# Mixer B's intra-chunk products: six halving levels in place of token pairs and far blocks

## The chip, the cores and the metric

The kernel runs on one core of a Trainium2 chip. The metric is device time in microseconds (us) for one launch; everything is float32. TensorE multiplies, VectorE (DVE) and ScalarE (ACT) work element by element, GpSimd has little to do, and SyncE's queue (SP) issues nearly all loads.

## The reference, cut to what matters

Two layers (`DEPTH`), each with 1024 tokens and 1024 channels. One projection of the normalised input feeds four token mixers A to D; their outputs are projected, weighted by gates, summed and added to the residual. The change is inside mixer B alone, a gated linear recurrence with 4 heads of 64 channels, in chunks of 64 tokens:

```
bcum = cumsum(log_f) inside the chunk
att[t, s] = sum_d q[t, d] * k[s, d] * exp(bcum[t, d] - bcum[s, d])      for s <= t
o = att @ v + (q * exp(bcum)) @ state
state = exp(b_last) * state + (k * exp(b_last - bcum))^T @ v
```

The exponent depends on the token pair and on the channel, so `att` is no plain product of two matrices. It becomes one if a reference position r with s <= r <= t is put between: exp(bcum[t] - bcum[r]) scales q and exp(bcum[r] - bcum[s]) scales k, and both factors are at most 1.

## The kernel before, in words

**Order of the work.** The mixers run in the order C, D, B, A, each with a stream of instructions per engine; a stage of B begins on TensorE when D's outputs have been turned. The heads of B are worked in two halves m (two heads e each, on partitions 64e to 64e+63); chunks c lie in pairs, one tile i of 128 tokens (8 tiles).

**Filler.** `pe_fill(pe, n)` puts n matmuls of later projections (128x128 weights, 512 columns; each matmul is two instructions in the trace, L368 and L365) into TensorE's queue between dependent steps. The list `FILL_ORDER` is fixed and in order: projections for D, gate blocks, projections for B, more gate blocks, projections for A, gate blocks. 8 matmuls make a piece, which ScalarE copies out of one of two PSUM banks; 4 pieces make a block of weights, which SyncE loads two blocks ahead. What is left of the list when mixer A ends is run at the start of the last stage (`pe_tail`, L456). `D_FILL`, `B_FILL` and `ATT_FILL` say how many matmuls stand at each place. In B they are 16 three times ("start"), then in each half 3 before each of 16 pair steps, 1 ("near"), 1 ("far"), 2 and 1 in each of 8 tiles, and at last 16 ("turn"), 212 in all.

**Mixer B before.** After VectorE's running sums (`log_cum`) each half goes through these steps:
1. Pairs within 16 tokens. For each offset s in 0..15 VectorE subtracts (L1272), ScalarE exponentiates (L1197), VectorE multiplies by q and k (L1290, L1292) over 1024 - 64 s elements, in two buffers `ee`, and TensorE sums over the channels with a selector matrix (L1099). ScalarE copies the sums (L1199), TensorE transposes them.
2. State additions. VectorE scales the keys to the chunk's end (L1295, L1297), TensorE transposes them (L1116), ScalarE copies (L1207), TensorE multiplies with the values (L1123), VectorE runs a chain of 15 steps for the states (L1304).
3. For each tile VectorE places the pair sums (L1316), TensorE brings them into PSUM with the identity (L1133) and adds the far blocks of 16 tokens (L1137), VectorE masks (L1321), TensorE multiplies with the values (L1147) and adds the product of queries and state (L1150), ScalarE copies (L1210).

At the end VectorE normalises and gates (L1327 to L1335) and TensorE turns the result (L560). Mixer A begins with `pe_fill_until`, then its projection (L341); its VectorE part first waits for a bias table that SyncE builds by three DMAs in turn, once B has ended (L798 to L803).

Of the kernel before, what the change touches and what calls it, by code (L numbers as in the profile page):

```python
# [8 lines left out]
ALU = mybir.AluOpType  # L9
# [10 lines left out]
SUB = 16  # L20
NSUB = CH // SUB
# [22 lines left out]
B_FILL = {"start": 16, "pairs": 3, "far": 1, "attT": 2, "oB": 1, "turn": 16, "near": 1}  # L44
# [9 lines left out]
for _n, _w in PARAM_SIZES:  # L54
# [3 lines left out]
CONST_SIZES = [("ident", 128), ("head_sum", 128), ("pair_sel", 62), ("strict_c", 64),  # L58
               ("incl_t", 128), ("incl_c", 64), ("lv0", 64), ("lv1", 64), ("lv2", 64), ("lv3", 64), ("lv4", 64), ("lv5", 64),
               ("lv0_t", 64), ("sub_diag", 128), ("chunk_neg", 128), ("rot", 128), ("ones", 64), ("diag2", 64)]  # L60
# [6 lines left out]
def constants():  # L67
# [12 lines left out]
    put("pair_sel", np.concatenate([np.zeros((P, 30)), (t // HD) == np.arange(2)[None, :], np.zeros((P, 30))], 1))  # L80
    put("incl_t", same & (s >= t))
# [6 lines left out]
    put("sub_diag", ((t // SUB) == (s // SUB)) & (s <= t))  # L88
# [78 lines left out]
def gated_merge_kernel(nc, x, w_in, w_branch, w_out, params, toep, consts, cos_sin, a_mask, final_g, out):  # L167
    ctx = ExitStack()
    jobs = Jobs()
    with ctx:  # L170
# [886 lines left out]
        def mixer_b():  # L1057
            q, key, bc, v, z = bq_raw, U(0), bf_raw, b_v, V(2)
            o_rows = H(14.5, 2).rearrange("p (m i c) -> p m i c", m=2, i=NT)
            qt, qh, kj = H(4), H(5), [H(6), H(7), H(8)]  # L1060
            khn = H(9).rearrange("p (i c) -> p i c", i=NT)
            ee = [H(10), H(11)]
            near = H(12, 0.25).rearrange("p (i j e) -> p i e j", i=NT, e=2)
            st = H(12.5, 1.0625).rearrange("p (c v) -> p c v", c=17)
            near_x = H(12.25, 0.25).rearrange("p (e s) -> p e s", e=2)
            att_t = [H(13.5625 + 0.25 * n, 0.25).rearrange("p (e t) -> p e t", e=2) for n in range(2)]
# [14 lines left out]
            def subs(x):  # L1081
                return x.rearrange("p (c j t) -> p c j t", j=NSUB, t=SUB)

            def pe(pe):
# [4 lines left out]
                for m in range(2):  # L1089

                    ap = jobs.open(pe, ("near", m), S2[0])
                    for s in range(SUB):
                        pe_fill(pe, B_FILL["pairs"])
                        pe.wait_ge(sg("pairs_ready"), SUB * m + s + 1)
                        for half in range(2):

                            x = ee[s % 2][:, 512 * half:512 * half + 512].rearrange("p (b t) -> p b t", t=SUB)[:, :, s:]
                            o = ap[0:2 * SUB, 512 * half:512 * half + 512].rearrange("p (b t) -> p b t", t=SUB)[:, :, s:]
                            ins = pe.matmul(o, lhsT=C("pair_sel")[:, 2 * (SUB - 1 - s):2 * (2 * SUB - 1 - s)], rhs=x,  # L1099
                                            start=s == 0, stop=True, skip_group_check=True)  # L1100
                        jobs.mark(("pairs", m, s))
                        if s < SUB - 1:
                            ins.then_inc(sg("pairs_summed"), 1)
                    jobs.filled(ins, ("near", m))
                    pe_fill(pe, B_FILL["near"])
                    jobs.stored(pe, ("near", m))
                    ap = jobs.open(pe, ("nearT", m), O)
                    for i in range(NT):
                        ins = pe.transpose(ap[:, 2 * SUB * i:2 * SUB * i + 2 * SUB], ee[1][0:2 * SUB, P * i:P * i + P],
                                           ident[0:2 * SUB, 0:2 * SUB])  # L1110
                    jobs.filled(ins, ("nearT", m))

                    ap = jobs.open(pe, ("khn", m), S2[1])
                    pe.wait_ge(sg("end_keys"), m + 1)
                    for i in range(NT):
                        ins = pe.transpose(ap[:, P * i:P * i + P], ee[0][:, P * i:P * i + P], ident)  # L1116
                    jobs.filled(ins, ("khn", m))
                    jobs.stored(pe, ("khn", m))
# [7 lines left out]
                    pe_fill(pe, B_FILL["far"])  # L1126
                    pe.wait_ge(sg("far_ready"), m + 1)
                    for i in range(NT):
                        pe.wait_ge(sg("near_placed"), NT * m + i + 1)
                        ap = jobs.open(pe, ("attT", m, i), S2[0])  # L1130
                        for e in range(2):
                            o = ap[:, 512 * e:512 * e + P]
                            pe.matmul(o, lhsT=near_x[:, e, :], rhs=ident, start=True, stop=True, skip_group_check=True)  # L1133
                            for j in range(1, NSUB):
                                cols = o.rearrange("p (c j t) -> p c j t", c=2, j=NSUB)[:, :, j, :]
                                rhs = subs(qt)[HD * e:HD * e + HD, 2 * i:2 * i + 2, j, :]
                                ins = pe.matmul(cols, lhsT=kj[j - 1][HD * e:HD * e + HD, P * i:P * i + P], rhs=rhs,  # L1137
                                                start=False, stop=True, skip_group_check=True)
                        jobs.filled(ins, ("attT", m, i))
                        pe_fill(pe, B_FILL["attT"])  # L1140
                        if i == 0:
                            pe.wait_ge(sg("states_" + str(m)), 1)
                        jobs.stored(pe, ("attT", m, i))
                        ap = jobs.open(pe, ("oB", m, i), S2[1])
                        for e in range(2):
                            vv = v[:, i, HD * (2 * m + e):HD * (2 * m + e) + HD]
                            pe.matmul(ap[:, 512 * e:512 * e + HD], lhsT=att_t[i % 2][:, e, :], rhs=vv, start=True, stop=True, skip_group_check=True)  # L1147
                            for c in range(2):
                                t0 = P * i + CH * c
                                ins = pe.matmul(ap[CH * c:CH * c + CH, 512 * e:512 * e + HD], lhsT=qh[HD * e:HD * e + HD, t0:t0 + CH],  # L1150
                                                rhs=st[HD * e:HD * e + HD, 2 * i + c, :], start=False, stop=True, skip_group_check=True)
                        jobs.filled(ins, ("oB", m, i))
                        pe_fill(pe, B_FILL["oB"])
# [4 lines left out]
            def act(act):  # L1158
# [22 lines left out]
                for m in range(2):  # L1181
                    b = bc[:, m, :]
                    if m:
                        act_ready(act, ("oB", 0, NT - 1))
                    act.activation(qh, b, ACT.Exp).then_inc(sg("qh_exp"), 1)
                    act.wait_ge(sg("qt_diff"), m + 1)
                    act.activation(subs(qt)[:, :, 1:, :], subs(qt)[:, :, 1:, :], ACT.Exp).then_inc(sg("qt_exp"), 1)
                    for j in range(1, NSUB):
                        act.wait_ge(sg("kj_diff"), 3 * m + j)
                        x = chunks(kj[j - 1])[:, :, 0:SUB * j]  # L1190
                        act.activation(x, x, ACT.Exp).then_inc(sg("kj_exp"), 1)
                    for s in range(SUB):
                        if s >= 2:
                            act_fills(act, ("pairs", m, s - 2))
                        act.wait_ge(sg("pair_diff"), SUB * m + s + 1)
                        x = ee[s % 2].rearrange("p (b t) -> p b t", t=SUB)[:, :, s:]
                        act.activation(x, x, ACT.Exp).then_inc(sg("pair_exp"), 1)  # L1197
                    ap = act_ready(act, ("near", m))
                    jobs.emptied(act.activation(ee[1][0:2 * SUB, :], ap[0:2 * SUB, :], ACT.Copy), ("near", m))  # L1199
                    ap = act_ready(act, ("nearT", m))  # L1200
                    if m:
                        jobs.ready(act, ("attT", 0, NT - 1))
                    jobs.emptied(act.activation(H(12, 0.25), ap[:, 0:256], ACT.Copy), ("nearT", m))
                    act.wait_ge(sg("end_diff"), m + 1)
                    act.activation(ee[0], ee[0], ACT.Exp).then_inc(sg("end_exp"), 1)
                    ap = act_ready(act, ("khn", m))
                    jobs.emptied(act.activation(H(9), ap, ACT.Copy), ("khn", m))  # L1207
                    for i in range(NT):
                        ap = act_ready(act, ("oB", m, i))
                        jobs.emptied(act.activation(o_rows[:, m, i, :].rearrange("p (e v) -> p e v", e=2),  # L1210
                                                    ap.rearrange("p (e v) -> p e v", e=2)[:, :, 0:HD], ACT.Copy), ("oB", m, i))
# [5 lines left out]
            def dve(dve):  # L1217
# [34 lines left out]
                for m in range(2):  # L1252
                    b, qq, kk = bc[:, m, :], q[:, m, :], key[:, m, :]

                    if m:
                        jobs.ready(dve, ("oB", 0, NT - 1))
# [615 lines left out]
```

## Time and profile before

| what | value |
|---|---|
| median of 3 runs | 3810.22 us (3809.53 to 3810.95) |
| the profiled execution's own time | 3809.59 us |
| its span | 3807.8 us |
| mean granted TensorE clock | 0.960 of 2.4 GHz |
| TensorE busy | 3507.4 us (92%) |
| VectorE busy | 1695.2 us (45%) |
| ScalarE busy | 690.3 us (18%) |
| GpSimd busy | 60.9 us (2%) |

The span is the time from the first to the last instruction; the execution's time is 1.8 us longer. A busy TensorE isn't TensorE at its peak, since its clock has two levels and small products leave most of the array idle.

### The profile page before, as it was taken

How to read it: one execution, taken by the hardware profiler on the slowest of the kernel's cores; microseconds unless marked ns; L12 is line 12 of the kernel's file. 1: busy time of each engine (PE TensorE's matmuls, PEld its weight loads, DVE VectorE, ACT ScalarE, POOL GpSimd, SP SyncE). 2: the span in 40 equal slices, each digit the busy share in tenths (PEclk: the TensorE clock that was granted, in tenths of full speed). 3: DMA queues.
4: the chain of work that ended last, by engine and by line, in shares of the span. 5: the costliest groups of instructions: out<-in, count | busy, mean ns of one | idle time of the engine just before them, and what ended most of it. 6: DMA issues, size and time to landing. Idle time of an engine off the chain costs nothing. (4 is left out here: it accounts for less than half of the span.)

```text
span 3807.8 us, 42754 instructions
## 1 busy us (share of the span) xinstructions
PE 3507.4 (92%) x17400; PEld 1764.5 (46%) x17400; DVE 1695.2 (45%) x3604; ACT 690.3 (18%) x1334; POOL 60.9 (2%) x52
## 2 busy tenths in 40 slices
PE   7999979999998998999989999789999899899997
PEld 3343545455543453554443345454555344546443
DVE  1179952722365321226112899446323734212442
ACT  2031023200122111310111310232101312113000
POOL 0003000000000000000000110000000000000000
PEclk9999989999998999999999999999999889899999
DMA  4101110100010012035031011000011101020531
GB/s 165 36 11 45 52 40 17 33 13 26 29 59 25 25 39 86 28 120 176 0 114 36 23 38 65 23 20 31 13 32 40 42 28 42 30 82 25 185 108 50
DMA packets 132334, 195.53 MB, mean 51 GB/s; under 512 B 8072, under 2 KB 87976, under 8 KB 131880
## 3 DMA queue, kind: packets, MB, share of 16 engines
q1 hardware_dynamic: 113544, 158.67, 12.9%
q10 hardware_dynamic: 18592, 34.09, 2.5%
q8 instruction: 140, 2.29, 0.3%
q14 instruction: 58, 0.48, 0.0%
HBM read 146.07 MB, written 48.78 MB: 51 GB/s over the span
## 5 line engine op out<-in xcount | busy, mean ns | idle before, releaser
L368 PE MATMUL ps<-hT,wr 128*128 128x512 f32 x3008 | 1445.0, 619 | 28.0 <-DMA wr<-in_w_in 10.4
L368 PEld LDWEIGHTS ps<-hT,wr 128*128 128x128 f32 x3008 | 549.7, 195 | 613.6 <-issue 573.1
L1031 DVE TENSOR_SCALAR_CACHE_REDUCE arena<-arena,sm 128x384 f32<-128x384 f32 (+5 forms) x384 | 337.9, 943 | 2.2
L758 DVE CUSTOM_DVE_ANT_0 arena<-ps,arena 128x640 f32<-128x640 f32 (+7 forms) x128 | 90.6, 708 | 373.8 <-PE ps L702 373.7
L341 PE MATMUL ps<-wr,hT 128*128 128x512 f32 x512 | 225.0, 601 | 15.2 <-DVE arena L629 15.2
L325 PE MATMUL ps<-hT,wr 128*128 128x512 f32 x512 | 224.6, 600 | 0.0
L466 PE MATMUL ps<-xo,arena 128*128 128x512 f32 x512 | 220.2, 592 | 1.7 <-ACT gts L408 1.7
L478 PE MATMUL ps<-wr,hT 128*128 128x512 f32 x512 | 220.1, 592 | 0.0
L1438 PEld LDWEIGHTS ps<-arena 64*64 64x64 f32 x4096 | 139.2, 135 | 135.0 <-issue 65.2
L365 PE MATMUL ps<-wr,hT 128*128 128x256 f32 (+1 forms) x512 | 192.2, 510 | 6.5 <-DMA wr<-in_w_in 6.5
L715 PEld LDWEIGHTS ps<-arena 128*128 128x128 f32 x1056 | 137.2, 193 | 82.0 <-issue 76.0
L408 ACT ACTIVATE gts<-ps 128x512 f32<-128x512 f32 x128 | 76.0, 596 | 507.5 <-PE ps L368 507.1
L1438 PE MATMUL ps<-arena 64*64 64x64 f32 (+1 forms) x4096 | 165.1, 227 | 0.0
L341 PEld LDWEIGHTS ps<-wr,hT 128*128 128x128 f32 x512 | 98.9, 194 | 141.3 <-issue 124.4
L325 PEld LDWEIGHTS ps<-hT,wr 128*128 128x128 f32 x512 | 98.3, 193 | 127.0 <-issue 127.0
L466 PEld LDWEIGHTS ps<-xo,arena 128*128 128x128 f32 x512 | 97.1, 190 | 124.8 <-issue 124.8
L478 PEld LDWEIGHTS ps<-wr,hT 128*128 128x128 f32 x512 | 97.3, 190 | 122.5 <-issue 122.5
L737 ACT ACTIVATE arena<-arena,sm 128x640 f32<-128x640 f32 (+7 forms) x128 | 94.1, 735 | 302.6 <-DVE sm L763 302.6
L715 PE MATMUL ps<-arena 128*128 128x64 f32 x1056 | 134.3, 271 | 11.0 <-DVE arena L775 9.8
L692 PE MATMUL ps<-con,arena 128*128 128x128 f32 x528 | 99.1, 292 | 41.7 <-ACT arena L737 34.9
L365 PEld LDWEIGHTS ps<-wr,hT 128*128 128x128 f32 x512 | 90.6, 191 | 39.6 <-issue 27.4
L1099 PE MATMUL ps<-arena,con 128*32 128x512 f32 (+15 forms) x256 | 78.1, 430 | 30.2 <-DVE arena L1292 30.0
(270 smaller groups left out, 3245.9 us busy)
## 6 DMA issues: line engine op xcount, KB each, us to landing
wr<-in_w_in SPq DMA_DIRECT2D x68, 1024.0 KB, 5.7
gate_tanh<-gts ACTq DMA_DIRECT2D x128, 256.0 KB, 2.0
arena<-gate_tanh SPq DMA_DIRECT2D x128, 256.0 KB, 2.9
x_cur<-arena SPq DMA_DIRECT2D x2, 4096.0 KB, 17.0
arena<-in_w_branch SPq DMA_DIRECT2D x8, 1024.0 KB, 8.7
wr<-in_w_out SPq DMA_DIRECT2D x8, 1024.0 KB, 6.1
arena<-x_cur SPq DMA_DIRECT2D x4, 2048.0 KB, 8.0
arena<-in_x SPq DMA_DIRECT2D x4, 1024.0 KB, 7.9
```

Source lines behind the costliest of these rows:

```text
L325: ins = pe.matmul(ap, lhsT=wr[:, n % 2, kt, P * m:P * m + P], rhs=hT[:, kt, 512 * half:512 * half + 512], start=kt == 0, stop=kt == KT - 1)
L341: ins = pe.matmul(o, lhsT=hT[:, kt, P * i:P * i + P], rhs=wr[:, n % 2:n % 2 + nb, kt, :], start=kt == 0, stop=kt == KT - 1)
L365: ins = pe.matmul(ap[:, 0:NCB * nb].rearrange("p (a c) -> p a c", a=nb), lhsT=hT[:, kt, P * c:P * c + P], rhs=wr[:, slot:slot + nb, kt, :] ...
L368: ins = pe.matmul(ap, lhsT=wr[:, slot, kt, P * m:P * m + P], rhs=hT[:, kt, 512 * c:512 * c + 512], start=kt == 0, stop=kt == KT - 1)
L466: ins = pe.matmul(ap, lhsT=wbs[ORDER.index(b)][:, k2, P * ct:P * ct + P], rhs=xo[:, 2 * ORDER.index(b) + k2, 512 * half:512 * half + 512], ...
L478: ins = pe.matmul(ap[:, 512 * j:512 * j + 512].rearrange("p (a c) -> p a c", a=2), lhsT=yT[:, kt, P * i:P * i + P], rhs=wr[:, 2 * j:2 * j ...
L692: ins = pe.transpose(ap[:, P * j:P * j + P], rows[u % 2][:, P * (g + j):P * (g + j) + P], ident)
L715: ins = pe.matmul(o[:, HD * h:HD * h + HD], lhsT=probs_t[u % 2][:, P * j:P * j + P], rhs=v[:, k0 + j, HD * h:HD * h + HD], start=j == 0, s ...
L737: act.activation(r, r, ACT.Exp, bias=neg[:, u % 2:u % 2 + 1], accum_out=tot[:, u % 8:u % 8 + 1]).then_inc(sg("probs_" + b), 1)
L758: ins = dve.tensor_tensor_reduce(out=rows[u % 2][:, 0:P * nb], in0=ap[:, 0:P * nb], in1=bias(i, h, nb), scale=HD ** -0.5, scalar=-3e38, op ...
L1031: ins = dve.tensor_scalar(compared[i], iscore[i], cbits[:, j:j + 1], None, ALU.is_ge, ALU.add, accum_out=count[:, j:j + 1])
L1438: ins = pe.matmul(ap[rows, c0 + width * h:c0 + width * h + width], lhsT=left[rows, h, :], rhs=right[rows, h, :], start=True, stop=True)
```

## The change

The chunk of 64 tokens is halved six times (`LEVELS = 6`). At level n it lies in blocks of 2h tokens, h = 32, 16, 8, 4, 2, 1. With the block's last token of the first half as reference, the second half of q and the first half of k are scaled and lie side by side in one buffer of 1024 columns, `scaled[n]`. The product of the buffer with itself, 64x64 for each head and chunk, has the pairs (s in the first half, t in the second half of one block) among others that a mask removes. A seventh product of plain keys and queries gives the diagonal. VectorE masks all seven (`near7`) and sums over them into `att_t`. TensorE keeps the output of all 8 tiles in two PSUM banks (`T`, `O`, one per head): first the products of queries and states, then for each tile the values. ScalarE copies each bank once per half. The end keys come first now, with their own buffer `ek`. TensorE's loop over the tiles puts in turn: the seven products of tile i, one matmul of filler, the values of tile i - 1. Filler in B is 3 x 16, in each half 6 + 2 + 16 and 8 x 1, and 16 at the end: 128 in all.

```diff
-B_FILL = {"start": 16, "pairs": 3, "far": 1, "attT": 2, "oB": 1, "turn": 16, "near": 1}
+B_FILL = {"start": 16, "end": 6, "khn": 2, "adds": 16, "att": 1, "turn": 16}
+            scaled = [H(4 + n) for n in range(LEVELS)]
+            qh, ek = H(10), H(12)
+            def second(x, lv):
+                return x.rearrange("p (b n t) -> p n b t", n=2, t=CH >> (lv + 1))[:, 1]
...
             def pe(pe):
...
                 for m in range(2):
+                    pe_fill(pe, B_FILL["end"])
+                    ap = jobs.open(pe, ("khn", m), S2[1])
+                    pe.wait_ge(sg("end_keys"), m + 1)
+                        ins = pe.transpose(ap[:, P * i:P * i + P], ek[:, P * i:P * i + P], ident)
+                    pe_fill(pe, B_FILL["khn"])
...
+                    pe_fill(pe, B_FILL["adds"])
+                    pe.wait_ge(sg("qh_ready"), m + 1)
+                    pe.wait_ge(sg("states_" + str(m)), 1)
...
+                    pe.wait_ge(sg("scaled_ready"), m + 1)
+                    for i in range(NT + 1):
+                        if i < NT:
+                            ap = jobs.open(pe, ("att", m, i), S2[i % 2])
+                            for n in range(LEVELS + 1):
+                                left, right = (scaled[n], scaled[n]) if n < LEVELS else (key[:, m, :], q[:, m, :])
+                                for e in range(2):
+                                    for c in range(2):
+                                        d, t0, c0 = slice(HD * e, HD * e + HD), P * i + CH * c, 512 * e + CH * n
+                                        ins = pe.matmul(ap[CH * c:CH * c + CH, c0:c0 + CH], lhsT=left[d, t0:t0 + CH],
+                                                        rhs=right[d, t0:t0 + CH], start=True, stop=True)
+                            pe_fill(pe, B_FILL["att"])
+                        pe.wait_ge(sg("att_ready"), NT * m + i)
...
              def act(act):
...
                 for m in range(2):
+                    act.activation(ek, ek, ACT.Exp).then_inc(sg("end_exp"), 1)
+                    for n in range(LEVELS):
+                        act.wait_ge(sg("level_diff"), LEVELS * m + n + 1)
+                        act.activation(scaled[n], scaled[n], ACT.Exp).then_inc(sg("level_exp"), 1)
+                        if n == 1:
+                            ap = act_ready(act, ("khn", m))
+                            jobs.emptied(act.activation(H(11), ap, ACT.Copy), ("khn", m))
+                            act.activation(qh, bc[:, m, :], ACT.Exp).then_inc(sg("qh_exp"), 1)
 ...
             def dve(dve):
...
                 for m in range(2):
+                    def level_diff(n):
+                        half = CH >> (n + 1)
+                        mid = b.rearrange("p (b t) -> p b t", t=2 * half)[:, :, half - 1:half].broadcast_to([P, S // (2 * half), half])
+                        dve.tensor_tensor(second(scaled[n], n), second(b, n), mid, ALU.subtract)
+                        dve.tensor_tensor(first(scaled[n], n), mid, first(b, n), ALU.subtract).then_inc(sg("level_diff"), 1)
+                    for n in range(LEVELS):
+                        if n + 1 < LEVELS:
+                            level_diff(n + 1)
+                        dve.wait_ge(sg("level_exp"), LEVELS * m + n + 1)
+                        dve.tensor_tensor(second(scaled[n], n), second(scaled[n], n), second(qq, n), ALU.mult)
+                        ins = dve.tensor_tensor(first(scaled[n], n), first(scaled[n], n), first(kk, n), ALU.mult)
+                    dve.tensor_tensor(qh, qh, qq, ALU.mult).then_inc(sg("qh_ready"), 1)
...
                     for i in range(NT):
+                        ap = jobs.ready(dve, ("att", m, i))
...
+                        ins = dve.tensor_tensor(masked, ap.rearrange("p (e n t) -> p e n t", e=2, t=CH)[:, :, 0:LEVELS + 1], each, ALU.mult)
+                        jobs.emptied(ins, ("att", m, i))
+                        jobs.stored(dve, ("att", m, i))
...
+                        dve.tensor_reduce(att_t[i % 2], masked.rearrange("p e n t -> p e t n"), AX, ALU.add).then_inc(sg("att_ready"), 1)
```

## Rows read from the trace of the kernel before

**Rows 1.** The page's busy times: engine, us, share of the span, instructions.
```profile
PE 3507.4 (92%) x17400; PEld 1764.5 (46%) x17400; DVE 1695.2 (45%) x3604; ACT 690.3 (18%) x1334; POOL 60.9 (2%) x52
```

**Rows 2.** Stretches: us, busy time of each engine (instructions), PEclk, DMA share, GB/s.
```profile
1107.20:1443.88 336.68, 306.63 (x1161) 151.85 (x1161) 150.31 (x237) 70.47 (x108) 0.00 (x0) 0.91 0.10 34
2984.51:3321.21 336.70, 306.68 (x1162) 151.87 (x1161) 150.29 (x237) 70.46 (x108) 0.00 (x0) 0.91 0.10 34
...
1220.00:1240.00 20.00, 12.65 (x105) 9.01 (x105) 7.52 (x21) 3.96 (x5) 0.00 (x0) 0.59 0.04 14
```

**Rows 3.** The filler of L368 alone in the first of these stretches.
```profile
1107.20:1443.88 336.68, 208.15 (x424) 77.69 (x424) 0.91 0.10 34
```

**Rows 4.** TensorE in order of time: start us, us, instructions; the last stage's filler.
```profile
1666.55 20.77 PE L368 MATMUL ps<-hT,wr 128*128 128x512 f32 x48
```

**Rows 5.** TensorE in order of time in mixer B, [idle before <-releaser].
```profile
1107.20 45.90 PE L368 MATMUL ps<-hT,wr 128*128 128x512 f32 x102
1158.43 3.62 PE L1099 MATMUL ps<-arena,con 128*32 128x512 f32 x4 [5.33 <-DVE arena L1292]
...
1227.87 1.99 PE L1123 MATMUL ps<-xo,arena 64*64 64x64 f32 x64 [1.11 <-ACT arena L1207]
...
1235.28 0.77 PE L1133 MATMUL ps<-con,arena 128*128 128x128 f32 x2 [3.42 <-DVE arena L1316]
```

**Rows 6.** The page's groups: busy us, mean ns of one, idle before.
```profile
L1438 PE MATMUL ps<-arena 64*64 64x64 f32 (+1 forms) x4096 | 165.1, 227 | 0.0
...
L1099 PE MATMUL ps<-arena,con 128*32 128x512 f32 (+15 forms) x256 | 78.1, 430 | 30.2 <-DVE arena L1292 30.0
```

**Rows 7.** TensorE in order of time in mixer D, one tile's products.
```profile
837.73 0.85 PE L1411 MATMUL ps<-con,arena 128*128 128x128 f32 x6 [1.14 <-DVE arena L1645]
838.51 0.46 PE L1422 MATMUL ps<-arena 64*64 64x64 f32 x16
838.79 0.41 PE L1422 MATMUL ps<-xo,arena 64*64 64x64 f32 x16
...
840.90 1.98 PE L365 MATMUL ps<-wr,hT 128*128 128x512 f32 x4
842.82 1.15 PE L1438 MATMUL ps<-arena 64*64 64x64 f32 x32
```

**Rows 8.** ScalarE in order of time in mixer B: copies of transposes and of a tile.
```profile
1226.79 1.02 ACT L1207 ACTIVATE arena<-ps 128x1024 f32<-128x1024 f32 x1 [3.38 <-PE ps L1116]
...
1263.52 0.28 ACT L1210 ACTIVATE arena<-ps 128x128 f32<-128x128 f32 x1 [5.95 <-PE ps L1150]
```

**Rows 9.** VectorE in order of time in mixer B: the states, the normalisation.
```profile
1229.99 4.71 DVE L1304 SCALAR_TENSOR_TENSOR arena<-arena,sm,ps 128x64 f32<-128x64 f32 x15 [5.25 <-PE ps L1123]
...
1429.61 2.29 DVE L1327 TENSOR_TENSOR arena<-arena 128x2048 f32<-128x2048 f32 x1 [2.87 <-ACT arena L1210]
...
1439.78 2.36 DVE L1335 TENSOR_TENSOR arena<-arena 128x1024 f32<-128x1024 f32 x2
```

**Rows 10.** VectorE's groups by shape: busy us, mean ns, idle before.
```profile
L1328 DVE TENSOR_REDUCE sm<-arena 128x32 f32<-128x2048 f32 x1 | 2.3, 2286 | 0.0
...
L1292 DVE TENSOR_TENSOR arena<-arena 128x512 f32<-128x512 f32 x1 | 0.7, 691 | 0.0
...
L1292 DVE TENSOR_TENSOR arena<-arena 128x256 f32<-128x256 f32 x1 | 0.4, 425 | 0.0
...
L1292 DVE TENSOR_TENSOR arena<-arena 128x64 f32<-128x64 f32 x1 | 0.3, 275 | 0.0
```

**Rows 11.** The start of mixer A in order of time, TensorE and VectorE.
```profile
1450.95 7.77 PE L368 MATMUL ps<-hT,wr 128*128 128x512 f32 x12
...
1476.46 3.03 DVE L821 SCALAR_TENSOR_TENSOR arena<-arena 128x640 f32<-128x640 f32 x4 [34.32 <-DMA arena<-a_bias_table]
...
1479.87 43.10 PE L341 MATMUL ps<-wr,hT 128*128 128x512 f32 x96 [7.42 <-DVE arena L629]
```

**Rows 12.** TensorE in order of time in mixer D: filler after its weights.
```profile
924.93 2.05 PE L368 MATMUL ps<-hT,wr 128*128 128x512 f32 x2 [5.26 <-DMA wr<-in_w_in]
```

More of the change, by code:

```diff
@@ L19 @@
 CH = 64
-SUB = 16
-NSUB = CH // SUB
+LEVELS = 6
 HD = 64
@@ L79, in constants @@
     put("head_sum", same)
-    put("pair_sel", np.concatenate([np.zeros((P, 30)), (t // HD) == np.arange(2)[None, :], np.zeros((P, 30))], 1))
-    put("incl_t", same & (s >= t))
     tc, sc = t % CH, np.arange(CH)[None, :]
@@ L87, in constants @@
         put(f"lv{lv}", ((tc // (2 * b)) == (sc // (2 * b))) & ((tc // b) % 2 == 1) & ((sc // b) % 2 == 0))
-    put("sub_diag", ((t // SUB) == (s // SUB)) & (s <= t))
+    halves = [CH >> (n + 1) for n in range(LEVELS)]
+    put("near7", np.concatenate([((tc // (2 * b)) == (sc // (2 * b))) & ((tc // b) % 2 == 0) & ((sc // b) % 2 == 1)
+                                 for b in halves] + [tc == sc], 1))
     put("chunk_neg", np.where((t // CH) < (s // CH), -BIG, 0.0))
@@ L1059, in mixer_b @@
             o_rows = H(14.5, 2).rearrange("p (m i c) -> p m i c", m=2, i=NT)
[L1060 to L1066, printed above, removed]
+            scaled = [H(4 + n) for n in range(LEVELS)]
+            qh, ek = H(10), H(12)
+            khn = H(11).rearrange("p (i c) -> p i c", i=NT)
+            st = H(13, 1.0625).rearrange("p (c v) -> p c v", c=17)
+            att_t = [H(14.0625 + 0.125 * n, 0.125).rearrange("p (e t) -> p e t", e=2) for n in range(2)]
+            masked = H(21.25, 0.875).rearrange("p (e n t) -> p e n t", e=2, n=LEVELS + 1)
             bc_flat = H(16.5, 2)
@@ L1089, in pe @@
                 for m in range(2):
[L1091 to L1111, printed above, removed]
+                    pe_fill(pe, B_FILL["end"])
+                    jobs.mark(("B end", m))
                     ap = jobs.open(pe, ("khn", m), S2[1])
@@ new lines, in pe @@
+                    pe_fill(pe, B_FILL["adds"])
+                    jobs.mark(("B adds", m))
+                    o = [jobs.open(pe, ("oB", m, e), bk) for e, bk in enumerate((T, O))]
+                    pe.wait_ge(sg("qh_ready"), m + 1)
+                    pe.wait_ge(sg("states_" + str(m)), 1)
+                    for i in range(NT):
+                        for c in range(2):
+                            t0 = P * i + CH * c
+                            for e in range(2):
+                                ins = pe.matmul(o[e][CH * c:CH * c + CH, CH * i:CH * i + CH], lhsT=qh[HD * e:HD * e + HD, t0:t0 + CH],
+                                                rhs=st[HD * e:HD * e + HD, 2 * i + c, :], start=i == 0, stop=True, skip_group_check=True)
@@ L1181, in act @@
                 for m in range(2):
[L1182 to L1199, printed above, removed]
@@ L1212, in act @@
+                    act_fills(act, ("B adds", m))
+                    for i in range(NT):
+                        act_fills(act, ("B att", m, i))
+                    for e in range(2):
+                        ap = act_ready(act, ("oB", m, e))
+                        ins = act.activation(o_rows[:, m, :, HD * e:HD * e + HD], ap.rearrange("p (i v) -> p i v", i=NT), ACT.Copy)
+                        jobs.emptied(ins, ("oB", m, e))
                 act.wait_ge(sg("b_square"), 1)
@@ new lines, in dve @@
+                    r = chunks(b)[:, :, CH - 1:CH].broadcast_to([P, NCH, CH])
+                    dve.tensor_tensor(chunks(ek), r, chunks(b), ALU.subtract).then_inc(sg("end_diff"), 1)
+                    level_diff(0)
+                    dve.wait_ge(sg("end_exp"), m + 1)
+                    dve.tensor_tensor(ek, ek, kk, ALU.mult).then_inc(sg("end_keys"), 1)
+                    for n in range(LEVELS):
[4 more added lines that the diff above has]
+                        ins = dve.tensor_tensor(first(scaled[n], n), first(scaled[n], n), first(kk, n), ALU.mult)
```

127 lines of the change are left out of this document (32 added, 95 removed).

## The prediction

> **What bounds the kernel now.** I read the page's busy times first, then the stretches of mixer B, then the order in which TensorE works there, then the other engines at the places where it waits.
>
> TensorE is busy for 92% of the span and VectorE for 45% [rows 1], so TensorE's queue sets the time and I price only what shortens or lengthens that queue. Mixer B is the stretch from the end of mixer D's turns to the start of B's own: 336.68 us in the first layer, 336.70 us in the second [rows 2]. One layer is worked out and doubled.
>
> Much of B is filler: 424 instructions of later projections [rows 3], two to each call counted by `pe_fill`. At the higher level of the clock one takes 0.43 us (48 in 20.77 us [rows 4]), so 424 are 182 us; the trace has 208 us, because part of them ran at the lower clock. The other 155 us of B (336.7 minus 182) are B's own products, waits, and time at the lower clock. Around 1220 to 1240 us the granted clock averages 0.59 of 2.4 GHz and TensorE is idle for 7 of 20 us [rows 2]. The waits are on VectorE's pair products and then on its chain of states, 5.33 us and 3.42 us in the shown half [rows 5]. The pair sums alone are 256 instructions and 78.1 us in both layers [rows 6]. In the loop over tiles one tile takes 6.2 us (0.28 + 5.95 us between ScalarE's copies [rows 8]): VectorE masks, TensorE multiplies, each waiting for the other, with filler between.
>
> **What goes, per layer.** All pair sums (39 us), the transposes of their result, the far products and the masks at full width. The 336.7 us are replaced as a whole, so nothing is subtracted twice.
>
> **What comes, per layer, in TensorE's order.** The filler of the opening is kept: 102 instructions took 45.9 us [rows 5], of which the last 6 stood ahead of the first pair sums. The new opening has 12 ("end") in their place: 45.9 + 6 x 0.43 = 48.5 us.
>
> Each half m then has:
> - 8 transposes of the scaled end keys. Six took 0.78 us to the next start [rows 7], so 1.0 us.
> - 2 fills, 1.7 us. ScalarE's copy of the transposes takes 1.02 us [rows 8] and lies beside them.
> - 32 products that add to the states, 64 instructions. The price is that of mixer D's 64x64 products which go around all four quarters of the array: 16 instructions in 0.28 us, 0.0175 us each [rows 7]. 1.1 us, and 0.2 us for the change from filler to 64x64 (four instructions of filler, 1.72 us at 0.43, took 1.92 us to the next start [rows 7]): 1.3 us.
> - 16 fills, 13.8 us, to hide VectorE's work. VectorE is held at level 2, whose exponential stands behind the copy and `qh`'s on ScalarE: about 3.2 us after the transposes, by three instructions over 1024 elements, some 1.02 us each [rows 8]. Behind it are six pairs of 512-wide operations (two 0.69 us operations overlap to 1.22 us [rows 10]), 7.3 us, `qh` 1.1 us and the chain of 15 states 4.7 us [rows 9]: 16.3 us after the transposes. TensorE arrives after 1.7 + 1.3 + 13.8 = 16.8 us. Level 5 works on single elements; by the reading below that may add up to 1.5 us. I put 1.0 us of waiting into the sum (bounds 0 and 2).
> - 32 products of queries with states, 1.1 + 0.2 = 1.3 us.
> - The loop over 8 tiles, below: 24.6 us.
>
> That is 1.0 + 1.7 + 1.3 + 13.8 + 1.0 + 1.3 + 24.6 = 44.7 us, twice 89.4 us. The second half also has 6 fills of "end", 5.2 us; the first half's are in the opening. The turns come last: 16 fills, 13.8 us. VectorE's normalisation took 12.5 us from the first square to the gated rows [rows 9], and before it come two ScalarE copies of some 0.6 us, so 14.2 us in all.
> B after: 48.5 + 89.4 + 5.2 + 14.2 = 157.3 us, 179.4 us less than before.
>
> **The loop over tiles** decides most of the uncertainty. TensorE has 56 instructions for the seven products of both heads and chunks (1.0 us), two fill instructions (0.86), one change (0.2) and 8 instructions for the values. The last use two quarters, of which 32 instructions took 1.15 us [rows 7], so 0.3 us. Together 2.4 us. VectorE has one mask over 896 elements and one sum over the seven levels. From 512 and 256 elements (691 and 425 ns [rows 10]) an element costs 1.04 ns and an instruction 0.16 us: the mask is 1.09 us. A contiguous sum of 2048 took 2.29 us [rows 10], so 896 would be 1.09 us as well. This sum steps 64 elements at each read. The nearest row for single elements is the last pair product: 64 elements, each alone in 16, took 275 ns where the line through the others gives 225 [rows 10], 0.78 ns more per element. If all of that is due to the step, the sum takes 1.09 + 0.70 = 1.8 us; if it is a floor for short operations, 1.09 us. I take 1.7 us, near the stepped row's end, since this sum steps farther still. With two waits of VectorE on itself, 0.04 us each, a tile is 2.9 us, VectorE's and not TensorE's. Eight tiles 23.2 us, the first products 1.0 and the last values 0.4: 24.6 us. Bounds: 2.4 us (TensorE's) and 3.6 us a tile (a sum at twice the row's extra cost), which is -16 and +22 us over 32 tiles.
> The Trainium skill ("Vector Engine (DVE) Microarchitecture Reference", section 5.2) says that a port keeps its rate only for runs of two adjacent words, and gives 1.73 ns per element for one source hopping every element, 2.50 for small steps. By it the sum would be an estimated 1.7 to 2.4 us. The 275 ns agree with the lower figure.
>
> **What moves.** The fills of B fall from 212 to 128, 168 instructions fewer. They don't go away: mixer A has its own fixed number, so they are run in the burst ahead of the last stage, where 48 took 20.77 us [rows 4]. And at A's start 12 instructions were run to end a piece, beside a wait that ended only when the bias table's DMA let VectorE go [rows 11]. The count after the change (256 in place of 424, modulo 16) leaves 4 to run there, so 8 more go to the end while the stall still ends where it did. 176 x 0.43 = 75.7 us per layer come back. ScalarE empties a piece of 16 in 0.6 us of their 6.9, so that nothing is late there; each weight block (64 instructions, 27 us) is asked for one block ahead.
>
> **Sum.** 179.4 - 75.7 = 103.7 us per layer, 207.4 us in both. The profiled execution took 3809.59 us (span 3807.8), so 3602.2 us; the median of the runs is 0.63 us above it. I predict 3603 us.
>
> **Rivals.**
> 1. *The clock sinks in the new loop.* For it: TensorE would be idle for about 0.5 us in every 2.9, and the one stretch with waits of several microseconds shows 0.59 [rows 2]. Against: the alternation of filler and 64x64 products in D has fills of 0.43 us, the full clock [rows 7], and no single gap of the new loop is long. At 1.2 GHz a tile is 56 x 0.031 us (64 instructions took 1.99 us right after a wait [rows 5]) + 1.7 of filler + 0.6 + 0.3 = 4.3 us, 1.4 us more: 32 tiles, +45 us, 3648 us. Chance 0.12. The Trainium skill ("TensorE: Matmul & The Clock Gate", "A second HAM failure mode: psum-queue depth-cycling") describes a kernel whose short pauses between groups were enough for this; no row here decides on it.
> 2. *The moved filler doesn't run at full rate.* In D one block came 5.26 us late, and two fill instructions then took 2.05 us [rows 12]. Some 2.75 blocks more stand at each layer's end; 7 us for each is +38 us, 3641 us. Against: there nothing else asks for DMA until the last block is loaded. Chance 0.07.
> 3. *The 64x64 products don't overlap* (slower than before). One lasts 0.227 us [rows 6]. One after another, a tile would need 64 x 0.227 + 0.9 = 15.4 us, 12.5 more, and the 512 state instructions of the run 0.2 us more each: +400 + 102, about 4105 us. It decides from about 0.1 us per instruction on (207 us over 2560 instructions, beside the loop's 0.5 us of slack). Against: the rows of D, with the same order of quarters and each row half in its own bank. Chance 0.03.
> 4. *VectorE's stepped operations cost more than my upper bound*, so that the states and the tiles are both late: 4.5 us a tile, +51 us, 3654 us. Chance 0.08.
>
> **Chances.** My forecast has 0.69, with a range of its own of 3585 to 3628 from the loop's bounds and the states' wait. 0.01 is for something that eats the whole gain without more. Four of five times the time should lie between 3578 and 3648. What can be told from no change is about 0.2%, 8 us: faster by more 0.95, within 0.01, slower by more 0.04.
>
> **What would show it.** Mixer B (to the start of its turns) should be near 157 us; a tile of the new loop 2.9 us, with TensorE waiting for the sum over levels each time; the seven products of a tile about 1.0 us; the states' wait under 2 us; the granted clock near 1 from the opening to the turns; and about 224 filler instructions in the burst before the last stage, at 0.43 us. Tiles of 2.4 us would show the sum to be cheap in spite of its steps. Wrong altogether would be a tile over 5 us, or a burst with waits on weights.

## The result, and the profile after

The changed kernel took **3605.58 us** (median of 4 runs, 3600.27 to 3608.24) beside 3809.88 us of the kernel before on the same chip (4 runs, 3807.33 to 3810.95). The ratio is 0.9463, 95% interval 0.9447 to 0.9479. The forecast was 3603 us. The profiled execution took 3600.27 us, 2.0 us less than the sum of the prediction (3602.2).

The page's busy times and its largest group, to be read beside [rows 1] and [rows 6]:

```profile
PE 3327.1 (92%) x18520; PEld 1670.2 (46%) x18520; DVE 1661.8 (46%) x3470; ACT 652.0 (18%) x1246; POOL 60.8 (2%) x52
...
L366 PE MATMUL ps<-hT,wr 128*128 128x512 f32 x3008 | 1409.7, 612 | 27.6 <-DMA wr<-in_w_in 10.0
```

TensorE's share is 92% as before. It has 1120 instructions more and 180 us less of busy time: the page's shares say nothing of the gain, only stretches do. Those of mixer B (end of D's turns to the start of B's), and the filler in the first, in the columns of [rows 2]:

```profile
1097.92:1254.62 156.70, 145.08 (x1553) 72.71 (x1553) 132.14 (x170) 44.85 (x53) 0.00 (x0) 0.97 0.13 41
2878.03:3036.62 158.59, 147.01 (x1553) 73.52 (x1553) 132.19 (x170) 44.85 (x53) 0.00 (x0) 0.96 0.13 41
...
1097.92:1254.62 156.70, 120.08 (x256) 48.26 (x256) 0.97 0.13 41
```

The whole difference, by stretch:

| stretch | before, layers 0 / 1 | after | difference | predicted |
|---|---|---|---|---|
| up to B (stages C and D, unchanged) | 1107.20 / 1067.19 | 1097.92 / 1073.95 | -9.3 / +6.8 | 0 |
| mixer B to its turns | 336.68 / 336.70 | 156.70 / 158.59 | -180.0 / -178.1 | -179.4 |
| B's turns to the branch products | 244.27 / 244.46 | 319.80 / 319.69 | +75.5 / +75.2 | +75.7 |
| branch products to the end of the layer | 229.17 / 242.13 | 229.66 / 242.19 | +0.5 / +0.1 | 0 |

The first row is not the change: C and D have the same instructions in both, and over the executions of this study they took 1090 us (granted clock 0.98) to 1112 us (0.95) in layer 0, with 98 to 101 us of waits each time. So the experiments are also read on one stretch without them: **from the start of D's last turn to the first branch product**, 581.5 and 581.7 us before, 477.0 and 478.7 after, 477.2 and 478.7 in another execution of the changed kernel. I call it the late stretch. Mixer B's own 156.7 and 158.6 us move as well with the clock: in the other execution they are 155.6 and 158.7.

The moved filler is in the burst ahead of the last stage, 224 instructions of 0.43 us without a wait, to be read beside [rows 4]:

```profile
1477.28 96.30 PE L366 MATMUL ps<-hT,wr 128*128 128x512 f32 x224
```

One half of B in TensorE's order (start us, us, instructions, [idle before]):

```profile
1097.92 47.67 PE L366 MATMUL ps<-hT,wr 128*128 128x512 f32 x108
1145.42 1.04 PE L1096 MATMUL ps<-con,arena 128*128 128x128 f32 x8
1146.29 1.88 PE L366 MATMUL ps<-hT,wr 128*128 128x512 f32 x4
1148.11 1.16 PE L1104 MATMUL ps<-xo,arena 64*64 64x64 f32 x64
1149.20 14.00 PE L366 MATMUL ps<-hT,wr 128*128 128x512 f32 x32
1163.13 1.16 PE L1117 MATMUL ps<-arena 64*64 64x64 f32 x64
1164.11 1.00 PE L1129 MATMUL ps<-arena 64*64 64x64 f32 x56
...
1185.51 0.45 PE L1142 MATMUL ps<-xo,arena 64*64 64x64 f32 x8 [0.59 <-DVE arena L1280]
1188.40 0.45 PE L1142 MATMUL ps<-xo,arena 64*64 64x64 f32 x8 [2.44 <-DVE arena L1280]
1188.78 7.11 PE L366 MATMUL ps<-hT,wr 128*128 128x512 f32 x12
...
1239.09 15.70 PE L366 MATMUL ps<-hT,wr 128*128 128x512 f32 x32
```

The products with the states (L1117) start with no wait. In the loop TensorE waits 0.59 us per tile for the sum over levels, and 2.44 us at the last tile, where nothing is left beside mask and sum. All waits of TensorE in B (us in total, times, longest) are for that sum:

```profile
PE ps L1142 <- DVE arena L1280: 11.6, 14, 2.4
```

VectorE, in order of time: the last level's products (L1253, L1254: every second element), the states, then mask and sum of a tile:

```profile
1155.47 0.69 DVE L1253 TENSOR_TENSOR arena<-arena 128x512 f32<-128x512 f32 x1
1156.08 0.69 DVE L1254 TENSOR_TENSOR arena<-arena 128x512 f32<-128x512 f32 x1
...
1158.01 4.71 DVE L1264 SCALAR_TENSOR_TENSOR arena<-arena,sm,ps 128x64 f32<-128x64 f32 x15
...
1171.02 1.09 DVE L1273 TENSOR_TENSOR arena<-ps,con 128x896 f32<-128x896 f32 x1
1172.15 1.68 DVE L1280 TENSOR_REDUCE arena<-arena 128x128 f32<-128x896 f32 x1
1173.93 1.09 DVE L1273 TENSOR_TENSOR arena<-ps,con 128x896 f32<-128x896 f32 x1
```

From mask to mask is 2.91 us. Two windows, in the columns of [rows 2]: the granted clock is full through the loop and falls after its last wait.

```profile
1163.00:1188.00 25.00, 19.69 (x585) 12.39 (x584) 21.82 (x16) 0.60 (x1) 0.00 (x0) 1.00 0.01 3
1188.80:1194.00 5.20, 5.20 (x10) 2.20 (x9) 5.04 (x8) 3.67 (x5) 0.00 (x0) 0.67 0.00 0
```

And B's last turns and the start of mixer A, which answers to [rows 11]. In the turns TensorE waits 0.47 us before every pair of transposes; the last pair takes 0.69 us in place of 0.44, and the four fill instructions behind them 0.80 us each (granted clock 0.55 from 1260.95 to 1264.40 us). The stall has grown from 7.42 to 11.41 us, and VectorE goes on, as before, when the bias table has landed. Behind the stall 18 instructions take 10.46 us, 0.58 each.

```profile
1260.04 0.44 PE L558 MATMUL ps<-con,arena 128*128 128x128 f32 x2 [0.47 <-ACT xo L634]
1260.95 0.69 PE L558 MATMUL ps<-con,arena 128*128 128x128 f32 x2 [0.47 <-ACT xo L634]
1261.44 3.19 PE L366 MATMUL ps<-hT,wr 128*128 128x512 f32 x4
1264.47 13.90 PE L339 MATMUL ps<-wr,hT 128*128 128x512 f32 x32
1289.78 10.46 PE L339 MATMUL ps<-wr,hT 128*128 128x512 f32 x18 [11.41 <-DVE arena L627]
...
1286.36 3.03 DVE L819 SCALAR_TENSOR_TENSOR arena<-arena 128x640 f32<-128x640 f32 x4 [33.56 <-DMA arena<-a_bias_table]
```

### The profile page after: what moved, and what is told of

Read it like the earlier page. It is cut to its first block and busy times, and to the rows that moved or that the text cites. A ratio compares the mean times of both kernels' runs of the same rounds, so it can differ in the third digit from the quotient of the medians.

```text
span 3598.5 us, 44750 instructions
## 1 busy us (share of the span) xinstructions
PE 3327.1 (92%) x18520; PEld 1670.2 (46%) x18520; DVE 1661.8 (46%) x3470; ACT 652.0 (18%) x1246; POOL 60.8 (2%) x52
## 5 line engine op out<-in xcount | busy, mean ns | idle before, releaser
L366 PE MATMUL ps<-hT,wr 128*128 128x512 f32 x3008 | 1409.7, 612 | 27.6 <-DMA wr<-in_w_in 10.0
L323 PE MATMUL ps<-hT,wr 128*128 128x512 f32 x512 | 226.0, 603 | 0.0
L489 DVE SCALAR_TENSOR_TENSOR hT<-arena,ps 128x512 f32<-128x512 f32 x32 | 22.0, 689 | 212.3 <-PE ps L464 212.3
```

What stands on the lines that cost most here:

```text
L323: ins = pe.matmul(ap, lhsT=wr[:, n % 2, kt, P * m:P * m + P], rhs=hT[:, kt, 512 * half:512 * half + 512], start=kt == 0, stop=kt == KT - 1)
L366: ins = pe.matmul(ap, lhsT=wr[:, slot, kt, P * m:P * m + P], rhs=hT[:, kt, 512 * c:512 * c + 512], start=kt == 0, stop=kt == KT - 1)
```

## The experiments

Nine runs were made, one of them the changed kernel itself once more. Three questions: is the gain where the working says (pair steps, 64x64 products), is the tile bound by VectorE's stepped sum, and what do the waits that are left cost, with and without the clock?

**1. The sum over levels reads adjacent elements** (what it sums is then not the seven levels of one pair).

```diff
-dve.tensor_reduce(att_t[i % 2], masked.rearrange("p e n t -> p e t n"), AX, ALU.add)
+dve.tensor_reduce(att_t[i % 2], masked_flat, AX, ALU.add)   # "p (e t n) -> p e t n"
```

> The changed kernel with one edit: VectorE's sum over the seven levels reads 896 adjacent elements instead of stepping 64 elements at each read (same count, other numbers are summed, so the sums over levels are left out of the result). Theory: the step costs the sum 0.6 us (1.68 us measured against 1.09 us for adjacent elements) and VectorE's tile of 2.91 us sets the loop; then a tile falls to TensorE's own 2.3 to 2.45 us, 32 tiles, 15 to 19 us less than the changed kernel: 3587 to 3591 us. Rival, the 1.68 us are the price of a sum with 7 elements to each output whatever the step: no change, 3605 us.

Measured: 3580.99 us (before 3819.78 there), ratio 0.9383 (0.9344 to 0.9422). VectorE's sum, and the end of TensorE's loop:

```profile
1168.15 1.09 DVE L1281 TENSOR_REDUCE arena<-arena 128x128 f32<-128x896 f32 x1
1170.47 1.09 DVE L1281 TENSOR_REDUCE arena<-arena 128x128 f32<-128x896 f32 x1
```

```profile
1183.20 0.45 PE L1143 MATMUL ps<-xo,arena 64*64 64x64 f32 x8 [1.28 <-DVE arena L1281]
1183.58 5.42 PE L366 MATMUL ps<-hT,wr 128*128 128x512 f32 x12
```

The step costs 0.6 us of the 1.68. A tile goes to 2.25 us, TensorE's own time, and the waits inside the loop vanish. The late stretch is 465.2 and 464.6 us, 26 us less over both layers; the waits account for some 18. Most of the rest is the clock, 2 x 1.7 us a layer: the 12 instructions behind the loop take 5.42 us and not 7.11, and B's last 32 take 14.00 and not 15.70. The second half's last wait is 1.58 us here, and the clock stays full behind it too.

**2. Two fills per tile in place of one.**

```diff
-B_FILL = {..., "att": 1, "turn": 16}
+B_FILL = {..., "att": 2, "turn": 16}
```

> The changed kernel with 2 matmuls of filler per tile of the new loop in place of 1. Theory: TensorE waits 0.59 us in each tile for VectorE, filler put there is taken from the burst before the last stage at 0.43 us an instruction, so per half 6.9 us leave the burst, the loop grows by 7 x 0.27 us (2.32 + 0.86 = 3.18 us a tile in place of 2.91) and its last wait of 2.4 us shrinks: 14 to 22 us less in all, 3584 to 3592 us. Rival, filler in the loop delays the next tile's products and so VectorE: a tile of 3.8 us, +0.9 x 32 - 27.5, no gain: 3605 to 3608 us.

Measured: 3581.39 us, ratio 0.9391 (0.9356 to 0.9426); late stretch 464.3 and 463.7 us, 28 less. A tile is 3.11 us without a wait, and the last wait has shrunk:

```profile
1194.11 0.45 PE L1142 MATMUL ps<-xo,arena 64*64 64x64 f32 x8 [0.64 <-DVE arena L1280]
1194.49 5.42 PE L366 MATMUL ps<-hT,wr 128*128 128x512 f32 x12
```

The working closes: 11.6 us of waits and 2 x 1.7 us of clock are gone per layer and 2 x 0.64 stay, which makes 13.7; the stretch shows 12.7 and 15.0. A slower loop made the kernel faster, because the fill has to be run somewhere.

**3. The products ordered quarter by quarter**: seven (14 instructions) in a row on one quarter of the array, in place of one on each in turn.

```diff
-for n in range(LEVELS + 1):
-    for e in range(2):
-        for c in range(2):
+for e in range(2):
+    for c in range(2):
+        for n in range(LEVELS + 1):
```

> The changed kernel with the same 28 products per tile in another order: all seven levels in one quarter of the array, then the next quarter, instead of going around the four quarters at each level. Theory: one quarter takes an instruction each 0.07 us (four quarters 0.0175 us each in turn, two quarters 0.034 us), so 56 instructions take 3.9 us in place of 1.0, a tile 5.2 us, 32 tiles +70 to +80 us: 3675 to 3685 us. Rival, TensorE takes an instruction each 0.0175 us in any order: 3605 us.

Measured: 3633.34 us, ratio 0.9524 (0.9491 to 0.9558); late stretch 495.8 and 496.0 us, 36 more.

```profile
1184.21 2.89 PE L1129 MATMUL ps<-arena 64*64 64x64 f32 x56
1188.09 0.45 PE L1142 MATMUL ps<-xo,arena 64*64 64x64 f32 x8
1188.37 2.89 PE L1129 MATMUL ps<-arena 64*64 64x64 f32 x56
```

56 products take 2.89 us in place of 1.00, a tile 4.16 in place of 2.91. The order of the quarters is worth a factor of three, 0.05 us an instruction against 0.017; my expectation, 0.07, was too high, and so its time. With 1.9 us more of products a tile grows by only 1.25 us, since 0.59 us of waiting goes. The last wait of the loop is 1.44 us, and the 12 fill instructions behind it take 5.42 us, which gives some of it back. The Trainium skill ("TensorEngine Tiling (Array Packing)", "Key Properties") says that different tiles of the array can load and multiply in parallel; that going around four quarters is faster agrees with it, by a factor of three here and not of four.

**4. The kernel before with one of 16 pair steps** (the other 15 steps of each half are left out, on all three engines; the fill of B's half stands ahead of them).

```diff
-for s in range(SUB):
+for s in range(PAIRS):        # PAIRS = 1
-B_FILL = {"start": 16, "pairs": 3, ...
+B_FILL = {"start": 16, "pairs": 48, ...
```

> The kernel before with only the first of its 16 pair steps (the pairs at other offsets are left out); its 48 matmuls of filler per half stand ahead of that step. It prices the pair steps alone. Theory: per half 19.5 us of sums, some 7 us of waits on VectorE and some 3 us of lower clock go, 4 halves, 105 to 125 us less than before: 3685 to 3705 us, so the pair steps are a little over half of the change's 204 us and the loop over tiles and the state steps the rest. Rival, the gain is the pair steps' nearly alone: 3630 us or less. Second rival, the pair steps' filler was what hid VectorE, and the waits come back: 3730 us or more.

Measured: 3706.86 us, ratio 0.9719 (0.9679 to 0.9760), late stretch 532.3 and 525.3 us, 106 less than before. So the pair steps are half of what the change saves in this stretch (207 us). The other half is what this run leaves in place, the state steps and the second loop. It was not divided by a run, only by rows. Ahead of the loop TensorE still waits, for 3.84 us at its start, and runs at the low clock behind that (4 fill instructions in 3.78 us):

```profile
1200.35 0.77 PE L1134 MATMUL ps<-con,arena 128*128 128x128 f32 x2 [3.84 <-DVE arena L1317]
...
1204.60 3.78 PE L369 MATMUL ps<-hT,wr 128*128 128x512 f32 x4
```

Inside the loop there is no wait at all. In the kernel before, two tiles in a row start 6.23 us apart, and all of TensorE's waits on L1316 in B are the two at the loops' starts:

```profile
1245.68 0.38 PE L1133 MATMUL ps<-con,arena 128*128 128x128 f32 x2
1251.91 0.39 PE L1133 MATMUL ps<-con,arena 128*128 128x128 f32 x2
PE ps L1133 <- DVE arena L1316: 6.8, 2, 3.4
```

Of the 6.23 us six fill instructions are 2.6, so a tile's own work was 3.65 us; in the new loop it is 2.91 - 0.86 = 2.05 us with its wait. By this estimate the loop is worth 1.6 us a tile, 51 us over 32 tiles, and the state steps, their waits and the clock the other 50.

**5. Four fills fewer ahead of the states' products.** Beside the kernels of 5, 6 and 7 the changed kernel ran once more on the same chip: 3614.42 us (3604.02 to 3628.18), ratio 0.9498 (0.9464 to 0.9532).

> The changed kernel itself, unchanged, as the base for the runs beside it on the same chip. Expected 0.946 of the kernel before.

```diff
-B_FILL = {..., "adds": 16, "att": 1, "turn": 16}
+B_FILL = {..., "adds": 12, "att": 1, "turn": 16}
```

> The changed kernel with 12 in place of 16 matmuls of filler ahead of the products with the states. Theory: VectorE's chain of states ends 0.4 us before TensorE arrives, so the 16 are just enough; 3.4 us less cover is 3.0 us of waiting per half, and if such a wait lets the clock fall (as the 2.4 us at the end of each loop seem to do) 1.7 us more; the 3.4 us of filler are run later at the same price. 4 halves: +12 us, with the clock +19 us. Rival, TensorE's queue has slack here and filler placed later costs the same as here: 0 us.

Measured: 3627.82 us, ratio 0.9508 (0.9481 to 0.9535). By the ratio that can't be told from the changed kernel; the late stretch shows it, 486.5 and 486.7 us, 17 more.

```profile
1177.49 1.99 PE L1117 MATMUL ps<-arena 64*64 64x64 f32 x64 [3.19 <-DVEq L1267]
1179.23 1.60 PE L1129 MATMUL ps<-arena 64*64 64x64 f32 x56
```

8 instructions of fill are 3.4 us, and 3.19 us of them come back as a wait: in the changed kernel VectorE was done only some 0.4 us before TensorE came. Four such waits are 12 to 13 us; the rest is the clock, for 64 instructions behind the wait take 1.99 us in place of 1.16 and the next 56 take 1.60 in place of 1.00. The version of the theory with the clock was right.

**6. Eighteen fills at A's start in place of two**, where the stall of 11.41 us was. Two of the eighteen end the piece, as before; sixteen are new, 32 instructions.

```diff
+A_FILL = 18
...
+pe_fill(pe, A_FILL)
```

> The changed kernel with 18 matmuls of filler at the start of mixer A (2 end the piece, 16 are new). Theory: TensorE waits 11.4 us there for VectorE, which waits for the bias table's DMAs, and that wait ends at a fixed time after B; 13.8 us of filler put ahead of A's projection come out of the later burst and replace the wait: 11.4 us less per layer and 2 us of lower clock at most, 18 to 26 us less in all. Rival, the wait moves along with TensorE's queue (the bias table is late by as much): no gain.

Measured: 3578.62 us, ratio 0.9378 (0.9362 to 0.9393); late stretch 464.8 and 462.8 us, 28 less.

```profile
1273.06 16.83 PE L367 MATMUL ps<-hT,wr 128*128 128x512 f32 x36
1289.72 10.46 PE L340 MATMUL ps<-wr,hT 128*128 128x512 f32 x24
```

The stall is gone, and 24 of A's products now take the time of 18, 0.44 us each in place of 0.58. So the gain is 11.4 us of stall and 18 x 0.14 = 2.6 us of clock per layer, 28 us in all. The stall is the bias table's: VectorE goes on when it has landed, 31.7 us after B's first turn in the changed kernel and 32.8 us here, where TensorE has 13.8 us more work ahead of its projection.

**7. Two more fills at the last tile of each half only.** It asks what makes the clock fall at the loop's end, the long wait there or all the 0.59 us waits together.

```diff
-pe_fill(pe, B_FILL["att"])
+pe_fill(pe, B_FILL["att"] + (2 if i == NT - 1 else 0))
```

> The changed kernel with 2 more matmuls of filler at the last tile of each half alone, where TensorE waits 2.4 us for the last sum. Theory: the wait falls to 0.7 us, which is 1.7 us per half, and the 12 filler instructions behind it take 5.4 us and not 7.1, because the clock no longer falls: 4 x 3.4 = 14 us less. Rival, the lower clock behind the loop comes from the loop's waits of 0.6 us and not from its end: 4 x 1.7 = 7 us less, and the 12 instructions still take 7.1 us.

Measured: 3582.40 us, ratio 0.9402 (0.9383 to 0.9422); late stretch 468.9 and 468.9 us, 18 less.

```profile
1173.95 0.38 PE L1142 MATMUL ps<-xo,arena 64*64 64x64 f32 x5 [0.59 <-DVE arena L1280]
...
1185.60 0.45 PE L1142 MATMUL ps<-xo,arena 64*64 64x64 f32 x8 [1.41 <-DVE arena L1280]
1185.98 5.42 PE L366 MATMUL ps<-hT,wr 128*128 128x512 f32 x12
```

The waits of 0.59 us before the end are still there and the clock stays, so they don't lower it; it is the loop's end. I had expected the last wait at 0.7 us; the 1.72 us of fill took 0.6 of the wait of the tile before it and 1.0 of the last. It isn't the work ahead of the wait either: in experiments 1 and 3 it is the same two fill instructions, the last waits are 1.28 to 1.58 us, and the fill behind them keeps its full rate (12 instructions in 5.42 us). But in all three runs the wait before the last has gone too, so the last wait by itself is not told from the last two together (0.59 + 2.44 us).

Gain by waits and clock in B, 2 x (1.6 + 1.7) = 6.6 us a layer; measured 8.1 and 9.8. The edit has a second effect that its expectation left out. Eight instructions more run in B, so 12 and not 4 end the piece at A's start, and the stall there shrinks from 11.41 to 8.53 us (8.62 in the second layer):

```profile
1256.19 6.60 PE L366 MATMUL ps<-hT,wr 128*128 128x512 f32 x12
1285.05 43.65 PE L339 MATMUL ps<-wr,hT 128*128 128x512 f32 x96 [8.53 <-DVE arena L627]
```

That is some 3 us of the gain in each layer, the same term that the prediction had for the eight instructions that leave A's start. In the first layer the opening took 0.9 us longer than in the changed kernel, which is the rest.

**8. Both: two fills per tile and eighteen at A's start.**

```diff
-B_FILL = {..., "att": 1, "turn": 16}
+B_FILL = {..., "att": 2, "turn": 16}
+A_FILL = 18
...
+pe_fill(pe, A_FILL)
```

> Two matmuls of filler per tile of the loop in place of one, and 18 matmuls of filler at the start of mixer A. Theory (TensorE has a fixed amount of filler to get through, and the two stalls, in the loop of B and at A's start, are in series and independent): the two gains add. From the end of D's turns to the last stage a layer took 477.2 and 478.7 us in the changed kernel, 464.3 and 463.7 with two matmuls per tile alone, 464.8 and 462.8 with A's filler alone; the sum of both gains gives about 451 and 448 us, 28 + 28 = 56 us less than the changed kernel in the whole, some 3550 to 3562 us, ratio to before 0.930 to 0.934. Rival (filler taken into the loop is missing from the tail, so that the tail's filler that runs beside mixer A's chains gives out and a wait returns there): one of the two gains is lost in part, 460 us and more a layer, 3575 us. In both, no wait in the loop above 0.1 us, no fall of the clock at the loop's end (12 filler instructions in 5.4 us), and no wait of 11.4 us at A's start.

Measured: **3545.03 us** (6 runs, 3532.57 to 3565.83), ratio 0.930 (0.9272 to 0.9328), the fastest of all. Late stretch 449.5 and 450.2 us: 56 less than the changed kernel, so the gains add, and the rival falls by which a wait would return for want of filler beside mixer A. In the columns of [rows 2], from the first fill of B to the branch products, the changed kernel and then this one:

```profile
1097.92:1574.42 476.50, 446.03 (x2542) 226.69 (x2541) 172.24 (x318) 112.64 (x221) 0.00 (x0) 0.97 0.16 55
```

```profile
1090.27:1539.29 449.02, 440.28 (x2541) 224.88 (x2541) 172.85 (x318) 112.75 (x221) 0.00 (x0) 0.99 0.17 58
```

The work is the same (2541 weight loads). The idle time has gone from 30.5 to 8.7 us, which is 21.7 of the 27.5; the other 5.8 us are the clock, 0.99 in place of 0.97.

## Why the prediction was right

Per layer, from the rows above; the sum was right to 2 us, of which the unchanged stages' clock makes 2.5, so that the change itself was missed by less than 1 us (-206.8 against -207.4). The mechanism held: a loop bound by VectorE's sum, cheap 64x64 products, moved filler at full rate. That the number is so close is luck, since mixer B alone took 155.5 to 158.7 us in three executions with the same code for it (the changed kernel twice, and experiment 6).

- **B as a whole**: 157.3 predicted, 156.7 and 158.6 measured. Its terms are not all right: -1.0 us in the opening, -1.4 in each half without its loop and +3.1 behind the loops nearly cancel.
- **Opening**: 48.5 predicted, 47.5 measured.
- **Half without the loop**: predicted 20.1, measured 18.7 (1145.42 to 1164.11). The *states' wait*, put at 1.0 us, did not come. VectorE was done 16.4 us after the transposes, as the step had it without the level 5 surcharge, and TensorE came at 16.8. The surcharge of up to 1.5 us is refuted: the products of level 5 take 0.69 us like those of [rows 10]. What I took for the cost of single elements in [rows 10], 275 ns at 64, is not one at a step of two elements. Experiment 5 shows how narrow this edge was: 0.4 us. (The six pairs of operations took 1.20 us each, from start to start, as the working needs them; [rows 10], which it names for 1.22, show durations only.)
- **Loop**: 24.6 predicted, 24.7 measured. A tile 2.9 and 2.91; the mask 1.09 and 1.09; the stepped sum 1.7 and 1.68 to 1.70; VectorE bounds it, shown by experiment 1. The 1.7 us were a good guess and in part luck. One figure for "single elements" was used for steps of 2 and of 64, and only the second costs; and the row of 275 ns may be what any short operation takes, for 64 adjacent elements of the state chain take 281 ns:

```profile
L1264 DVE SCALAR_TENSOR_TENSOR arena<-arena,sm,ps 128x64 f32<-128x64 f32 x60 | 16.9, 281 | 2.1
```

- **Products**: 1.0 us for 56, predicted from mixer D [rows 7], measured 1.00. Experiment 3 shows that this rests on the order of the quarters; rival 3 (no overlap) was the order, not the shape.
- **End and turn fills**: 5.2 + 14.2 predicted, 7.0 + 15.5 measured, 3.1 us more a layer. This is the step that failed. I looked at the loop for rival 1 and wrote that "no single gap of the new loop is long"; the last one is 2.44 us, it follows from my own numbers (mask, sum and nothing beside them), and the clock falls behind it. The turns' 14.2 us were given to VectorE, though the terms named for them make 12.5 + 1.2 = 13.7; VectorE was done 13.7 us after the loop, and TensorE's own fills, at the lower clock, took 15.5. Rival 1 priced +45 us for the loop; in the loop the clock stayed at 1.00. Its mechanism was real at the loop's end, for some 7 us over both layers, as experiments 1, 2 and 7 show.
- **What moves**: +75.7 predicted, +75.5 and +75.2 measured, 224 instructions in 96.3 us and no wait on weights (rival 2 falls). The stall at A's start grew by 4.0 us where eight instructions went away, as the step has it: those are paid twice, as idle time there and as fill in the burst. Experiment 7 shows the same from the other side.
- **Rival 4** falls with the 2.91 us tile.
- **The loop before** was read wrongly: "VectorE masks, TensorE multiplies, each waiting for the other". The 5.95 us of [rows 8] are ScalarE's idle time; TensorE had 6.2 us of work in each tile and no wait (experiment 4). The sum didn't use this reading, because it replaced B as a whole.

The Trainium skill was weighed twice ahead of the result. Its rule that a port keeps its rate only for runs of two adjacent words ("Vector Engine (DVE) Microarchitecture Reference", section 5.2) agrees with the trace at a step of 64, 1.68 us beside an estimated 1.7 by its lower figure. At a step of two elements the rule does not hold here: 512 elements took 0.69 us, as adjacent ones do. Its remark on short pauses ("TensorE: Matmul & The Clock Gate", "A second HAM failure mode: psum-queue depth-cycling") does not describe the inside of this loop, whose clock is 1.00 through the 0.59 us waits. It fits B's turns, where waits of 0.47 us before every 0.44 us of work end at the lower clock.

What stays open, and was not tried: why stages C and D run up to some 20 us apart between executions of the same code, from which step between 2 and 64 elements a VectorE read costs more, and whether one wait or the last two together lower the clock at the loop's end.

## What to carry to other kernels

When fill is a fixed number of instructions, price a change by what idle time it leaves, and look at the last iteration of a loop by itself: its wait has no cover, and the clock may charge for it behind the loop. After such a change, set the fill counts anew: two of them, two small edits, gave 56 us on top of 207. Count as well what a changed number does where a piece is ended. Order 64x64 products so that neighbours use different quarters of the array.

## What the runs showed of the hardware

- 64x64 f32 products: 0.017 us an instruction over four quarters in turn, 0.05 us with 14 in a row on one quarter.
- A VectorE sum over 896 elements takes 1.68 us at a step of 64 elements and 1.09 us at a step of one; a product of 512 elements takes 0.69 us at a step of two, as at one.
- The granted clock stayed at its full 2.4 GHz through waits of 0.59 us, one in each 2.9 us, and behind last waits of 1.41, 1.44 and 1.58 us; behind one of 2.44 us it fell (window at 0.67, between 1.2 and 2.4 GHz), and 12 instructions took 7.11 us in place of 5.42.
- In B's turns, with a wait of 0.47 us before each pair of transposes, the last pair took 0.69 us in place of 0.44, and four fill instructions behind them 3.19 us in place of 1.7.
